# Value projection with features as rows and a transpose, in a hybrid conformer and attention block

## What is computed

```python
u = rms_norm(h, g_pre_mix)                 # 2048 x 1024
z = u @ w_in                               # columns: GLU 1024 | q 512 | k 128 | v 128 | gates 2048
a, b = split(z_glu); c = causal_depthwise_conv(a * sigmoid(b), 31 taps)
y_conv = silu(layer_norm(c)) @ w_conv_out
q, k = rope(q), rope(k)                    # 8 query heads, 2 key/value heads of 64
y_attn = attention(q, k, v, sinks) @ w_attn_out   # chunks of 64 queries against 128 keys
h = h + rms_norm((sig(gA) * y_conv + sig(gB) * y_attn) @ w_out)
# then a gated feed-forward with a 3-tap convolution, and a per-layer embedding
```

## Time and profile before

| | |
|---|---|
| median of 3 runs | 3261.19 us |
| span of the profiled execution | 3260.9 us |
| TensorE busy | 2988.8 us (92%) |
| VectorE busy | 1990.7 us (61%) |
| ScalarE busy | 1290.6 us (40%) |
| GpSimd busy | 1193.5 us (37%) |
| mean granted TensorE clock | 0.949 |
| DMA | 86 GB/s mean |

### The profile page before, as it was taken

One profiled execution on the slowest core, in us unless ns is written; L12 is line 12 of the kernel. 1 busy time (PEld: TensorE's weight loads), 2 busy tenths in 40 slices (PEclk: granted clock), 3 DMA queues, 4 the chain that ended last, 5 costly groups with the idle time before them and its releaser, 6 DMA issues.

```text
span 3260.9 us, 42193 instructions
## 1 busy us (share of the span) xinstructions
PE 2988.8 (92%) x13232; PEld 2461.0 (75%) x13232; DVE 1990.7 (61%) x2535; ACT 1290.6 (40%) x2027; POOL 1193.5 (37%) x492
## 2 busy tenths in 40 slices
PE   7889899999888989999988898999989889899998
PEld 5777778877776777888777676788777767678876
DVE  7883567056789357705778835760678882675056
ACT  3453433234445343323444524332343542433234
POOL 3223344443322334444332243444434224344443
PEclk8789999999979999999997999999999799999999
DMA  3112222223311222222321122222232112222223
GB/s 103 59 47 82 88 84 96 97 97 110 98 52 58 78 87 85 97 96 96 116 92 57 47 85 86 90 97 97 92 121 92 46 58 84 81 90 97 97 96 104
DMA packets 93055, 279.99 MB, mean 86 GB/s; under 512 B 8576, under 2 KB 27264, under 8 KB 92928
## 3 DMA queue, kind: packets, MB, share of 16 engines
q1 hardware_dynamic: 76032, 269.98, 24.8%
q10 hardware_dynamic: 16896, 8.39, 0.9%
HBM read 269.95 MB, written 8.39 MB: 85 GB/s over the span
## 4 chain that ended last, share of the span: by engine, by line
issue 71%; POOL 16%; PE 10%; DVE 1%; POOLq 1%; ACT 0%; ACTq 0%; DVEq 0%
POOL w_lo L304 16%; PE ps L666 3%; PE ps L667 3%; PE ps L668 3%; POOLq L301 0%; DVE y_lo L1295 0%; POOLq L303 0%; DVE trig L995 0%; POOLq L304 0%; DVE ssum L1011 0%; DVE h L1202 0%; DVE h_tmp L1197 0%; DVE turns L991 0%; PE ps L921 0%; DVE f_tmp L1256 0%
## 5 line engine op out<-in xcount | busy, mean ns | idle before, releaser
L304 POOL TENSOR_TENSOR w_lo<-w_stage,w_hi 128x1024 fp32r<-128x1024 f32 x488 | 1193.3, 2446 | 2046.8 <-ACT w_hi L338 2046.4
L338 ACT ACTIVATE w_hi<-w_stage 128x1024 fp32r<-128x1024 f32 x488 | 516.4, 1059 | 993.5 <-PE ps L668 878.7
L666 PE MATMUL ps<-y_hi,w_hi 128*128 128x512 f32 x1536 | 606.9, 395 | 24.4 <-POOL w_lo L304 17.2
L667 PE MATMUL ps<-y_lo,w_hi 128*128 128x512 f32 x1536 | 601.5, 392 | 0.0
L668 PE MATMUL ps<-y_hi,w_lo 128*128 128x512 f32 x1536 | 601.3, 391 | 0.0
L1044 DVE SCALAR_TENSOR_TENSOR conv_acc<-conv_in,col,conv_acc 128x512 f32<-128x512 f32 x480 | 416.9, 938 | 2.6
L666 PEld LDWEIGHTS ps<-y_hi,w_hi 128*128 128x128 f32 x1536 | 290.5, 189 | 91.3 <-POOL w_lo L304 31.0
L668 PEld LDWEIGHTS ps<-y_hi,w_lo 128*128 128x128 f32 x1536 | 290.7, 189 | 61.3
L667 PEld LDWEIGHTS ps<-y_lo,w_hi 128*128 128x128 f32 x1536 | 290.8, 189 | 60.8 <-issue 1.0
L666 PE MATMUL ps<-u_hi,w_hi 128*128 128x512 f32 x800 | 319.9, 400 | 0.0
L667 PE MATMUL ps<-u_lo,w_hi 128*128 128x512 f32 x800 | 313.2, 392 | 0.0
(11 more groups left out here) (179 smaller groups left out, 4529.6 us busy)
## 6 DMA issues: line engine op xcount, KB each, us to landing
w_stage<-in_weights SPq DMA_DIRECT2D x488, 512.0 KB, 3.3
x_rows<-in_x SPq DMA_DIRECT2D x5, 2048.0 KB, 8.6
out_h<-ple ACTq DMA_DIRECT2D x32, 256.0 KB, 2.3
p_rows<-in_p SPq DMA_DIRECT2D x4, 512.0 KB, 5.5
pos_i<-in_positions SPq DMA_DIRECT2D x5, 256.0 KB, 5.5
col<-in_columns SPq DMA_DIRECT2D x1, 131.5 KB, 2.1
ident<-in_identity SPq DMA_DIRECT2D x1, 64.0 KB, 1.9
```

Source lines behind the costliest of these rows:

```text
L304: nc.gpsimd.tensor_tensor(w_lo[:, par], w_stage[:, par], w_hi[:, par].bitcast(F32), ALU.subtract).then_inc(w_lo_ready, 1)
L338: copy(w_hi[:, par], w_stage[:, par], ACT.Copy).then_inc(w_hi_ready, 1)
L666: nc.tensor.matmul(bank, w_hi[:, par, kk], hi, start=start, stop=False)
L667: nc.tensor.matmul(bank, w_hi[:, par, kk], lo, start=False, stop=False)
```

## The change

The value block becomes a `full_block` like the q and k blocks: w stationary, 512 tokens moving, 24 matmuls, features as rows in the same PSUM bank. ScalarE copies the bank to a new SBUF tile v_feat (128 x 512), TensorE transposes it in four pieces of 128 x 128 back into the same bank, and ScalarE copies from there as before. Two semaphores are new: v_out (copy done) and vt_done (transposes done).

```diff
+        v_feat = sb("v_feat", [P, T], F32)
@@ ScalarE
                 attend_q(0)
                 split_block(B_GA + 1)
                 done(B_QKV + PAIRS + 1)
+                copy(v_feat[:, :], ps[:, V_BANK], ACT.Copy).then_inc(v_out, 1)
+                act.wait_ge(vt_done, c + 1)
                 v_new = four(ps[:, V_BANK])
                 copy(v_even[CH:P, 0], v_even[CH:P, TT], ACT.Copy)
                 copy(v_odd[:, :, :], v_new, ACT.Copy).then_inc(v_step, 1)
@@ TensorE
-                ready(B_QKV + PAIRS + 1)
-                for t in range(TT):
-                    tok = slice(P * t, P * t + P)
-                    for k in range(8):
-                        nc.tensor.matmul(ps[:, V_BANK, tok], u_hi[:, k, tok], w_hi[:, 1, k], start=(k == 0), stop=False)
-                        nc.tensor.matmul(ps[:, V_BANK, tok], u_lo[:, k, tok], w_hi[:, 1, k], start=False, stop=False)
-                        last = nc.tensor.matmul(ps[:, V_BANK, tok], u_hi[:, k, tok], w_lo[:, 1, k], start=False, stop=(k == 7))
-                last.then_inc(block_done, 1)
+                full_block(B_QKV + PAIRS + 1, 1, V_BANK, u_hi, u_lo)
                 pe.wait_ge(rope_done, c * (PAIRS + 1) + 4)
...
+                def value_rows():
+                    pe.wait_ge(v_out, c + 1)
+                    for t in range(TT):
+                        last = nc.tensor.transpose(ps[:, V_BANK, P * t:P * t + P], v_feat[:, P * t:P * t + P], ident[:, :])
+                    last.then_inc(vt_done, 1)
+
                 scores(0)
+                value_rows()
                 with pe.Fori(0, SUB // 2 - 1) as i:
                     attend(i, True)
```

More of the change, by code:

```diff
@@ L241, in build_kernel @@
         glu_sig, glu_done, halo_in, conv_tap = map(sem, ("glu_sig", "glu_done", "halo_in", "conv_tap"))
-        rope_swapped, rope_step, rope_done, k_halo, v_step, v_ready = map(
-            sem, ("rope_swapped", "rope_step", "rope_done", "k_halo", "v_step", "v_ready"))
+        rope_swapped, rope_step, rope_done, k_halo, v_out, vt_done, v_step, v_ready = map(
+            sem, ("rope_swapped", "rope_step", "rope_done", "k_halo", "v_out", "vt_done", "v_step", "v_ready"))
         q_diag_ready, q_zeroed, v_cur_ready, qk_done, sm_step, sm_ready, exp_done, pn_ready, t_done, pt_ready, pv_done, \
```

## The result

| | before | after |
|---|---|---|
| median, us (4 runs each) | 3259.86 (3257.6 to 3261.84) | 3271.14 (3269.94 to 3274.53) |
| span of the profiled execution, us | 3260.9 | 3268.1 |
| mean granted TensorE clock | 0.949 | 0.951 |

The ratio is 1.0041, 95% interval [1.0028, 1.0053]: slower by 11.3 us by the medians and by 13.4 us by the ratio, so by about 3 us a chunk. A second measurement of the same two kernels gave 3273.54 against 3259.70, again 1.0041 [1.0028, 1.0054]. The ratios are not the quotients of the medians beside them, and differ from these by up to 0.0006. Medians and ratios are of the fast executions: one each of e3, e4 and the kernel before, at 5064.29, 3366.93 and 5933.6 us, is left out. The forecast was 3264 and "same"; what came is the second rival, priced at 3272.

A forecast was written before the change was run, and what follows sets the result against it. VectorE, not the value block, was taken to set when scores begin. Transposes +0.85 less clock relief 0.2 made +0.65 us a chunk, +2.6 in all; with 3260.9 + 0.3 that gave 3264 us, range 3257 to 3272.

The forecast's parts named there:

- the second rival: Before the second score maxima: ScalarE's lateness plus GpSimd's collision use up VectorE's idle time; about 2 us a chunk, 3272 us, 12%.
- The value block: TensorE ahead of the scores: block ends near 118.5 instead of 131.0 us, gain nothing, scores still at 135.38.
- The transposes and the clock: Between scores and first gate block: four transposes cost 0.85 us, clock relief returns 0.2, net +0.65 us a chunk.
- The strong clock rival: First gate block behind the transposes runs wholly at the lower clock: 5 us a chunk, 3281 us, 6%.
- Its mild form: Transposes do not carry the clock up, so no relief in the first gate block: +3.4 us, 3264.6 us, 15%.
- the relief of 0.2 us: First gate block: transposes take over part of the lower-clock time; half of 0.4 us, -0.2 us a chunk.
- ScalarE's lateness: ScalarE's value copies wait for the transposes, so the first exponentials and the work behind come some 4.4 us later.
- The failed step: VectorE's six taps before the second maxima: one GpSimd operation among them, 6.2 us, ending at 155.55, no price.
- point of decision: VectorE before the second maxima: a lateness 0.4 us larger than counted puts VectorE on the path.
- a cover: VectorE's 6.28 us of idle time before the second maxima absorbs the lateness, used up to some 0.4 us.

The follow-up runs named there:

- e3: Kernel before with only the value block changed to 24 matmuls of 512 columns, no v_feat copy or transposes (values in wrong layout): 3259.62 us, ratio 0.9992.
- e4: Changed kernel with ScalarE's first exponentials moved ahead of its wait for the transposes: 3261.95 us, ratio 1.0001 to the kernel before.
- e2: Kernel before plus four transposes into a free bank behind the first scores, waited for by nobody: 3259.83 us, ratio 0.9997.
- e1: Changed kernel with the transposes right behind the value block and ScalarE's value copies earlier: 3256.80 us, ratio 0.999 to the kernel before.
- e6: Kernel before, 96 short matmuls kept, plus four dummy transposes that ScalarE's value copies wait for: 3275.02 us, ratio 1.0047.
- e7: Changed kernel with GpSimd's two operations for the third and fourth gate blocks held until six taps are done: 3267.22 us, ratio 1.0026 to the kernel before.
- e9: Like e5, but third and fourth gate blocks split before the q_diag copies, GpSimd held until k_dup is written: 3251.89 us, 0.9977 to the kernel before.
- e5: Changed kernel with value transposes and first two gate blocks ahead of the scores, ScalarE's copies and split earlier: 3258.39 us, 0.9999 to the kernel before.

## Why the prediction was wrong

*The value block: right.* It ended 12.6 us earlier (118.6 against 131.2) and nothing came of it; the wait for q_diag went to 17 us and the scores to 135.32, as forecast, and e3 shows it alone.

*The transposes and the clock: right in size.* 0.71 us in TensorE's row, the later transposes 0.58 us late, forecast +0.65 a chunk. At the fourth maxima e2 has them at 0.6 us a chunk; over its whole run they are bounded at +2.3 us, and the middle is nothing. The strong clock rival is out: the gate matmuls are 0.23 us apart from 143.06 us on, and the two gate blocks take 11.8 us (141.28 to 153.06) where they took 12.0. Its mild form differs from my forecast by 0.8 us in all, which the time can't tell; in chunk 0 the relief of 0.2 us was there.

*ScalarE's lateness: right.* 4.46 us at the table load, 4.4 forecast.

*The failed step* is the sentence "GpSimd's operation is now due at 151.8, so I count 6.2: they end at 155.55", and what hung on it, "the price is nothing, but just so". I placed GpSimd's first operation right to 0.1 us and counted it once. Its second is due when ScalarE has split the next block, which waits for the end of the second gate block. By my own numbers that was 152.48 + 0.85 + 1.06 = 154.4, inside a group of taps that I had just lengthened to 155.55 (after: the split starts at 153.26 and takes 1.06, so 154.3). So one stall lengthens the group into the next one. 8.29 us instead of 6.2 put the maxima at 157.56 instead of 155.9, the idle time fell to nothing, and VectorE was on the path, to the second set of probabilities (4.52 us of waiting on TensorE). The rival named this mechanism, its place and its point of decision (0.4 us) and priced it, with the transposes, at 2.65 us a chunk and 3272 in all, near the 3271.14 measured. The nearness is part luck: the profiles show 2.1 us a chunk, transposes included, and the rest of the measured loss comes from elsewhere; I gave it 12% though only 0.4 us of 6.3 were left as a cover. e1, e4 and e6 show the lateness to be the cause, since taking it away removes the loss and adding it alone makes it. That the price is GpSimd's and VectorE's collision is shown by the rows, in which the stall moves with the operation (e7), and by e9 against e5: the same order of TensorE's work, ScalarE's splits and GpSimd's two operations moved ahead of the scores, and 14.2 us instead of 17.8 to the second maxima, 0.9977 instead of 0.9999. Late weights for the third gate block are no rival, as TensorE did not wait for them.

*What stays open.* The lateness and the collision explain 2.1 us a chunk; the two measurements give 2.8 to 3.5. Part of the rest can be the clock behind the fourth maxima: the changed kernel had one long stretch there in one profiled execution and three in the other, the kernel before one. Why the clock falls in one chunk and not in another, behind the same pause of 2.97 us, was not tried. Nor is it shown what gives lateness back outside the attention part: in the first profiled execution of after, k_dup began at 941.1 and 1750.2 us against 941.1 and 1750.6 before, then at 2559.5 against 2555.6.

## What to carry to other kernels

Where a cover comes out at a few tenths of a us after a shift, don't book it as free: walk the other engine's *next* operation through the lengthened stretch too, since a stall that lengthens a group of instructions invites the next one. And before shortening work on the engine with the largest busy share, read who it waits for behind that work: 12.5 us a chunk bought nothing here, and only became worth 6.7 us in all once the gate blocks filled the gap and GpSimd's operations were put where VectorE waits.

## What the runs showed of the hardware

- One GpSimd subtraction over 128x1024 (2.35 us) stops one VectorE instruction with two SBUF inputs for up to 2.2 us, at either size seen here: a 128x512 tap goes from 0.744 to 2.879 us, a 128x4 operation from 0.16 to 1.80 or 2.35 us. A reduction from PSUM beside it keeps its 0.69 us.
- GpSimd pays too: its two operations took 5.25 us among taps (5.62 in e5) and 4.66 us where VectorE was idle (e9).
- The kernel has its own scatter: with the same instructions the stretch from the fourth maxima to the token sums took 44.6 us in chunk 0 before and 41.9 to 42.1 in the others. The long one had a granted clock of 0.50 behind TensorE's pause of 2.97 us, the others 1.00. Over 48 such stretches (twelve profiled executions) all 19 long ones had 0.50 to 0.53 there. A loss of 2 us a chunk is hidden by this at the token sums of a single execution, and plain at a mark ahead of the pause.
